# Moving the on-chip tiles of a two-layer encoder to multiples of 512 bytes, and attention's value tiles to 320 bytes apart

## The chip, the cores and the metric

The kernel runs on one core of a Trainium2 chip. The metric is the device time of one execution in microseconds (us); three runs of the kernel before gave 4280.89, 4287.06 and 4291.22 us, so the median is 4287.06 us. The core has TensorE (matrix products, "PE", its weight loads "PEld"), VectorE ("DVE"), ScalarE ("ACT"), GpSimd ("POOL") and SyncE ("SP", which here issues most transfers). All tiles spoken of lie in the core's on-chip memory, which has 128 partitions; a tile has the same byte address in each partition, and "address" below means that one.

## The reference

Two layers, each of this form, over 2048 tokens of width 1024, all in float32:

```
h    = rmsnorm(x, norm_w[l])
proj = h @ w_in[l]                                  # 1024 -> 3344 columns
y_dn = deltanet(qkv, z, b, a)                       # 5-tap convolution, 4 heads of 128, both directions
y_at = attention(q, k, v, z)                        # 8 query heads, 2 key/value heads of 64, rotary positions
x    = x + concat(y_dn, y_at) @ w_out[l]            # 1024 -> 1024
```

and a last rmsnorm. The attention has softmax over all 2048 keys.

## The kernel before, in words

The kernel holds activations transposed: features on the partitions, tokens along them. It has three kinds of stages with products 512 tokens wide, and they make most of its TensorE work. In all three a float32 operand is split into a rounded part ("hi", type fp32r) and the rest ("lo", fp32r too), and three products (hi·hi, hi·lo, lo·hi) are summed in a bank of the accumulator memory.

1. **Input projection** (`input_projection`, line L328 of the profile). 26 weight tiles of 1024 x 128 a layer. For each tile and each half of the tokens, 8 k-steps of three terms, each term two products of 128x128 weights (`w_hi` or `w_lo`, "stationary") with 128x512 of `h_hi` or `h_lo` ("moving"): 96 products a tile. Tile 0 is done at lines L304 and L311, together with 128x32 weights `ba_w` for the gates. Beside it VectorE does the convolution (L516, L518) and the rotary products (L553 to L570), ScalarE evacuates (L408), GpSimd squares (L381), and TensorE sums squares between its products (L339, 448 pairs of small products over both layers).
2. **DeltaNet** (`delta_net`, L1039, L1047, L1064, L1072, L1115). A chunked recurrence over 16 chunks of 128 tokens in both directions. Its products are plain float32, 128 columns wide, and depend on each other across engines.
3. **Attention** (`attention`). 32 blocks a layer, each of 512 queries of one head. A block has 8 pairs of key tiles; TensorE does, for a pair, 4 score products (L1655 with `k1`, L1656 with `k2` of 68 rows, moving `q1`, `q2`), 6 value products (L1673: stationary `v_hi` or `v_lo`, 128x65, moving `p_hi` or `p_lo`), and 2 products for the next block's row maximum (L1628: stationary `q1`, moving `k1`). One small transpose (L1644) is added: 96 wide products and 1 small one a block. VectorE reads the maxima (L1743), splits the probabilities (L1761), and once a block does L1749, L1755 and L1767. ScalarE takes the exponential (L1730) and rounds (L1734).
4. **Output projection** (`output_projection`, L1890 and L1904). Products with the same shapes and types as those of L328: 128x128 weights `w_hi`/`w_lo`, moving 128x512 of `y_hi`/`y_lo`, two in a row with the same weights.

The order of all work is written out by hand; engines meet by semaphores. A max unit (L1628) may start when VectorE has read the unit two before it, since there are two banks for them.

Where a tile lies is decided by the order in which the tiles are made: each is put behind the last, its size rounded up to 32 bytes. The persistent tiles (`c_ident` and so on, in `build`) come first, the tiles of a stage behind them, and when a stage ends its room is used again. Before the change every fp32r product has its moving tile at a multiple of 64 bytes.

Of the kernel before, what the change touches and what calls it, by code (L numbers as in the profile page):

```python
# [7 lines left out]
P = 128  # L8
F32 = mybir.dt.float32
F32R = mybir.dt.float32r  # L10
# [4 lines left out]
SEQ = 2048  # L15
D_MODEL = 1024
DEPTH = 2
KT = D_MODEL // P
NC = SEQ // P
# [4 lines left out]
PADW = SEQ + CONV_K - 1  # L24
EPS = 1e-6

DN_HEADS = 4
N_DIR = 2
# [117 lines left out]
def input_projection(nc, a, c, l):  # L146
# [6 lines left out]
    with ExitStack() as stack, semaphores(nc, names) as s:  # L153
        b = Buffers(nc, stack, "proj")
        h_hi = b.sbuf("h_hi", [P, KT, SEQ], F32R)
        h_lo = b.sbuf("h_lo", [P, KT, SEQ], F32R)
        pad = b.sbuf("pad", [P, 2, PADW])
        out = b.sbuf("out", [P, 2, SEQ])
        w_raw = b.sbuf("w_raw", [P, 2, WCOLS])
        w_hi = b.sbuf("w_hi", [P, 2, KT, P], F32R)  # L160
        w_lo = b.sbuf("w_lo", [P, 2, KT, P], F32R)
        nw = b.sbuf("nw", [P, KT])
        sq = b.sbuf("sq", [P, SEQ])
        taps = b.sbuf("taps", [P, 2, WCOLS - KT * P])
        ba_raw = b.sbuf("ba_raw", [P, KT, W_BA])
        ba_w = b.sbuf("ba_w", [P, KT, 2 * W_BA], F32R)
        qk_w = b.sbuf("qk_w", [P, 6])
# [629 lines left out]
class Lanes:  # L797
# [3 lines left out]
    def __init__(self, b):  # L801
        self.raws = b.sbuf("lane_raw", [P, 2, BLK, BLK])
        self.mats = b.sbuf("lane_mat", [P, 2, BLK, BLK])
        self.invs = b.sbuf("lane_inv", [P, 2, BLK, BLK])
        self.tmp = b.sbuf("lane_tmp", [P, BLK * BLK // 4])
        self.beta = b.sbuf("lane_beta", [P, len(GROUP_STEPS), BLK])

# [27 lines left out]
def delta_net(nc, a, c, l):  # L835
# [6 lines left out]
    with ExitStack() as stack, semaphores(nc, names) as s:  # L842
# [9 lines left out]
                  for n in range(2))  # L852
        state = pair("state")
        norm = b.sbuf("norm", [P, 1])
        mean = b.sbuf("mean", [P, N_DIR, DN_HEADS])
        inv_mean = b.sbuf("inv_mean", [P, N_DIR, DN_HEADS])
        room = b.sbuf("room", [P, 12, N_DIR, DN_HEADS, P])
        r, se, oa, sq, ot, z, o, first_o, btc, y, am, kk = (room[:, n] for n in range(12))
# [656 lines left out]
K_ROWS = DH + NQ  # L1515


FIRST_BANKS = 6


def attention(nc, a, c, l):
# [15 lines left out]
    with ExitStack() as stack, semaphores(nc, names) as s:  # L1537
# [3 lines left out]
        v = b.sbuf("v", [P, NC, KV_HEADS, DH])  # L1541
        v_hi = b.sbuf("v_hi", [P, KV_HEADS, NC, DH + 1], F32R)
        v_lo = b.sbuf("v_lo", [P, KV_HEADS, NC, DH + 1], F32R)
        quarter = b.sbuf("quarter", [NQ, NQ, P])
# [10 lines left out]
        with nc.Block() as block:  # L1555
# [64 lines left out]
            def _(pe):  # L1620
# [38 lines left out]
                def values(j, slot, pair, first=False):  # L1659
# [9 lines left out]
                    for m in range(2):  # L1669
                        tile = 2 * pair + m  # L1670
                        for part_v, part_p in ((v_hi, p_hi), (v_hi, p_lo), (v_lo, p_hi)):
                            opens = tile == 0 and part_v is v_hi and part_p is p_hi
                            mm = nc.tensor.matmul(ps[0:DH + 1, 6 + kv, :], part_v[:, kv, tile, :], part_p[:, at, m, :],  # L1673
                                                  start=opens, stop=(tile == NC - 1 and part_v is v_lo))
# [379 lines left out]


FIRST_DIMS = [*range(0, DH // 4), *range(DH // 2, 3 * DH // 4)]
SECOND_DIMS = [d + DH // 4 for d in FIRST_DIMS]

# [31 lines left out]
def build(nc, a):  # L2090
# [6 lines left out]
    with ExitStack() as stack:  # L2097
        sb = lambda n, shape: stack.enter_context(nc.sbuf_tensor(n, shape, F32))
        c.ident = sb("c_ident", [P, P])
        c.ones = sb("c_ones", [P, P])  # L2100
        c.eps = sb("c_eps", [P, 2])
        c.quarters = sb("c_quarters", [P, 4])
        c.sums = sb("c_sums", [P, 2 * DN_HEADS, NC])
        c.tok = sb("c_tok", [P, TABLES, NC, ITEMS])
        c.v_scale = sb("c_v_scale", [P, NC, DN_HEADS])
        c.q_eps = sb("c_q_eps", [P, DN_HEADS, NC])
        c.sq_acc = sb("c_sq_acc", [P, SEQ])
        with semaphores(nc, "loaded set_up") as s:
# [88 lines left out]
```

## Time and profile before

| | |
|---|---|
| runs, median (lowest, highest) | 4287.06 (4280.89, 4291.22) us |
| span of the profiled execution, first to last instruction | 4274.5 us |
| what lies around the span, against the median | 12.6 us |
| TensorE busy | 3902.5 us, 91% of the span |
| VectorE, ScalarE, GpSimd busy | 2705.1, 1858.6, 671.4 us |
| mean granted TensorE clock | 0.956 |

No time is listed for the profiled execution other than its span. The profile gives each instruction's start and duration. For products the duration is a pipeline's latency and successive ones overlap, so what counts is the distance from one start to the next. In a timeline the same instructions in a row are merged: the start is that of the first, "x4" says how many. From the start of one row to the start of the next, divided by the count, is the distance.

### The profile page before, as it was taken

To read this page: it belongs to the slowest core of one execution; us is meant where nothing else is said; L and a number is where in the kernel's file an instruction comes from. 1 tells how busy PE (TensorE), PEld (TensorE's weight loads), DVE (VectorE), ACT (ScalarE), POOL (GpSimd) and SP (SyncE) were. 2 spreads that over 40 slices of the span, in tenths; PEclk is the share of its full clock that TensorE was granted. 3 is DMA by queue.
4 is the path that set the end of the run, shared out by engine and by line. 5 is a ranking of instruction groups with operands and counts; after the bars stand their busy time and mean duration, and the time that the engine had idled before them with its cause. 6 is when DMAs were issued, how large, how long until landed. Compare 5 with 4: busy or idle time off the path is not lost. (4 is left out here: it accounts for less than half of the span.)

```text
span 4274.5 us, 57577 instructions
## 1 busy us (share of the span) xinstructions
PE 3902.5 (91%) x19722; PEld 3081.4 (72%) x19722; DVE 2705.1 (63%) x3343; ACT 1858.6 (43%) x2599; POOL 671.4 (16%) x760
## 2 busy tenths in 40 slices
PE   4999998769979999998989999966997999999996
PEld 3788886569956666666768888855997666666674
DVE  5553035557779999985255420726776999999743
ACT  3222111335547777772133211112553777777611
POOL 0011100387510000000000111015864000000000
PEclk9999999889989999999989999988998999999997
DMA  6112145645550000005232121745455200000245
GB/s 248 67 59 74 59 152 187 159 104 141 144 164 25 23 25 23 22 14 175 113 113 74 59 74 59 237 128 130 130 154 145 109 25 23 25 22 24 67 161 221
DMA packets 338168, 423.04 MB, mean 99 GB/s; under 512 B 106248, under 2 KB 255880, under 8 KB 315600
## 3 DMA queue, kind: packets, MB, share of 16 engines
q1 hardware_dynamic: 335120, 399.93, 30.0%
q10 hardware_dynamic: 2880, 20.97, 1.2%
q8 instruction: 94, 1.54, 0.2%
q14 instruction: 74, 0.61, 0.0%
HBM read 272.89 MB, written 147.91 MB: 98 GB/s over the span
## 5 line engine op out<-in xcount | busy, mean ns | idle before, releaser
L1743 DVE TENSOR_REDUCE att_sb_part<-att_banks 128x1 f32<-128x512 f32 x992 | 681.1, 687 | 108.9 <-PE att_banks L1628 101.4
L1730 ACT ACTIVATE att_sb_probs<-att_banks 128x1024 f32<-128x1024 f32 x512 | 525.0, 1025 | 320.6 <-PE att_banks L1656 320.4
L1761 DVE TENSOR_TENSOR att_sb_p_lo<-att_sb_probs,att_sb_p_hi 128x1024 fp32r<-128x1024 f32 x512 | 622.3, 1215 | 19.1 <-ACT att_sb_p_hi L1734 18.9
L1734 ACT ACTIVATE att_sb_p_hi<-att_sb_probs 128x1024 fp32r<-128x1024 f32 x512 | 543.6, 1062 | 16.2
L328 PE MATMUL proj_banks<-proj_sb_h_hi,proj_sb_w_hi 128*128 128x512 f32 x1600 | 519.9, 406 | 6.2 <-DVE proj_sb_w_lo L476 6.2
L328 PE MATMUL proj_banks<-proj_sb_h_lo,proj_sb_w_hi 128*128 128x512 f32 x1600 | 516.7, 404 | 0.0
L328 PE MATMUL proj_banks<-proj_sb_h_hi,proj_sb_w_lo 128*128 128x512 f32 x1600 | 516.6, 404 | 0.0
L1039 PE MATMUL dn_banks<-dn_sb_room 128*128 128x128 f32 x3072 | 378.3, 283 | 57.4 <-DMA dn_sb_room<-proj 24.9
L1039 PEld LDWEIGHTS dn_banks<-dn_sb_room 128*128 128x128 f32 x3072 | 366.4, 198 | 79.8 <-DMA dn_sb_room<-proj 34.9
L1656 PE MATMUL att_banks<-att_sb_q,att_sb_k 68*128 68x512 f32 x1024 | 409.4, 400 | 0.0
L1655 PE MATMUL att_banks<-att_sb_q,att_sb_k 128*128 128x512 f32 x1024 | 407.6, 398 | 1.9 <-DVE att_sb_q L1755 1.9
L1673 PE MATMUL att_banks<-att_sb_p_hi,att_sb_v_hi 128*65 128x512 f32 x1024 | 404.1, 395 | 1.4 <-DVE att_sb_p_lo L1761 1.4
L1673 PE MATMUL att_banks<-att_sb_p_hi,att_sb_v_lo 128*65 128x512 f32 x1024 | 403.4, 394 | 0.0
L1673 PE MATMUL att_banks<-att_sb_p_lo,att_sb_v_hi 128*65 128x512 f32 x1024 | 402.9, 393 | 0.0
L1628 PE MATMUL att_banks<-att_sb_k,att_sb_q 128*128 128x512 f32 x992 | 400.2, 405 | 1.4 <-DVE att_sb_part L1743 1.4
L381 POOL TENSOR_TENSOR proj_sb_sq<-proj_sb_out 128x2048 f32<-128x2048 f32 x28 | 100.8, 3600 | 1882.9 <-ACT proj_sb_out L424 1316.9
L328 PEld LDWEIGHTS proj_banks<-proj_sb_h_hi,proj_sb_w_hi 128*128 128x128 f32 x1600 | 290.6, 190 | 65.4 <-issue 7.1
L328 PEld LDWEIGHTS proj_banks<-proj_sb_h_lo,proj_sb_w_hi 128*128 128x128 f32 x1600 | 292.6, 190 | 61.3
L328 PEld LDWEIGHTS proj_banks<-proj_sb_h_hi,proj_sb_w_lo 128*128 128x128 f32 x1600 | 292.4, 190 | 61.2
L476 DVE TENSOR_TENSOR proj_sb_w_lo<-proj_sb_w_raw,proj_sb_w_hi 128x1024 fp32r<-128x1024 f32 x52 | 69.0, 1327 | 412.2 <-ACT proj_sb_w_hi L403 412.2
L408 ACT ACTIVATE proj_sb_out<-proj_banks 128x1024 f32<-128x1024 f32 x56 | 57.5, 1026 | 545.3 <-PE proj_banks L328 545.3
L1628 PEld LDWEIGHTS att_banks<-att_sb_k,att_sb_q 128*128 128x128 f32 x992 | 189.8, 191 | 78.3 <-DVE att_sb_part L1743 5.1
(236 smaller groups left out, 5645.3 us busy)
## 6 DMA issues: line engine op xcount, KB each, us to landing
proj<-proj_sb_out SPq DMA_DIRECT2D x40, 1024.0 KB, 4.6
dn_sb_kq<-proj SPq DMA_DIRECT2D x64, 512.0 KB, 5.3
proj_sb_w_raw<-in_w_in SPq DMA_DIRECT2D x52, 516.0 KB, 5.1
dn_sb_room<-proj SPq DMA_DIRECT2D x32, 768.0 KB, 5.3
att_sb_q<-att_q SPq DMA_DIRECT2D x64, 256.0 KB, 3.0
ahead_delta<-x_res SPq DMA_DIRECT2D x16, 1024.0 KB, 6.7
x_res<-ahead_delta SPq DMA_DIRECT2D x16, 1024.0 KB, 4.2
proj_sb_pad<-proj SPq DMA_DIRECT2D x24, 512.0 KB
```

What stands on the lines that cost most here:

```text
L328: mm = nc.tensor.matmul(ps[:, 2 * half + n, :], w[:, u, k, :], h[:, k, at:at + QB], start=(k == 0 and w is w_hi and h is h_hi), stop=(k == ...
L381: nc.gpsimd.tensor_tensor(sq[:], out[:, u, :], out[:, u, :], ALU.mult).then_inc(s["squared"], 1)
L476: nc.vector.tensor_tensor(w_lo[:, u].rearrange("p k m -> p (k m)"), w_raw[:, u, 0:KT * P], w_hi[:, u].rearrange("p k m -> p (k m)").bitcas ...
L1039: mm = nc.tensor.matmul(out[:, h, :], left[:, h, :], right[:, h, :], start=True, stop=True)
L1628: nc.tensor.matmul(ps[:, 4 + u % 2, :], q1[:, slot, tile * P:(tile + 1) * P], k1[:, slot % 2, keys * QB:(keys + 1) * QB], start=True, stop ...
L1655: nc.tensor.matmul(out, k1[:, slot % 2, keys], q1[:, slot, :], start=True, stop=False)
L1656: mm = nc.tensor.matmul(out, k2[:, slot % 2, keys], q2[:, slot, :], start=False, stop=True)
L1673: mm = nc.tensor.matmul(ps[0:DH + 1, 6 + kv, :], part_v[:, kv, tile, :], part_p[:, at, m, :], start=opens, stop=(tile == NC - 1 and part_v ...
L1730: nc.scalar.activation(probs[:, pair % 2], ps[:, 2 * (pair % 2):2 * (pair % 2) + 2, :], ACT.Exp, scale=SCALE).then_inc(s["exp_done"], 1)
L1734: nc.scalar.activation(p_hi[:, pair % SLOTS], probs[:, pair % 2], ACT.Copy).then_inc(s["hi_done"], 1)
L1743: nc.vector.tensor_reduce(part[:, w // NQ, w % NQ:w % NQ + 1], ps[:, 4 + w % 2, :], AX.X, ALU.max) \
L1761: nc.vector.tensor_tensor(p_lo[:, pair % SLOTS], probs[:, pair % 2], p_hi[:, pair % SLOTS].bitcast(F32), ALU.subtract).then_inc(s["lo_done ...
```

## The change

No instruction is added, taken away or put elsewhere: with line numbers left out, the lists of instructions of the two kernels, engine by engine, are the same, word for word. Only addresses change. The persistent tiles get two fillers, `c_front` and `c_back`, so that `c_ident` and each stage's first tile start at a multiple of 512; in the projection, DeltaNet and the persistent group, tiles with odd sizes go behind the large ones; and a value tile of 65 columns gets room for 80 (`V_ROOM`), of which 65 are used.

| tile (use) | address before | modulo 512, 64 | address after | modulo 512, 64 |
|---|---|---|---|---|
| `proj_sb_h_hi` (moving) | 29376 | 192, 0 | 30208 | 0, 0 |
| `proj_sb_h_lo` (moving) | 94912 | 192, 0 | 95744 | 0, 0 |
| `proj_sb_w_hi` (stationary) | 201504 | 288, 32 | 177664 | 0, 0 |
| `proj_sb_w_lo` (stationary) | 209696 | 288, 32 | 185856 | 0, 0 |
| `proj_sb_ba_w` (stationary) | 226688 | 384, 0 | 202240 | 0, 0 |
| `proj_sb_pad` (convolution) | 160448 | 192, 0 | 212032 | 64, 0 |
| `dn_sb_room` (both) | 177568 | 416, 32 | 177664 | 0, 0 |
| `dn_sb_kq`, `dn_sb_state` | 156992, 173376 | 320, 0 | 157184, 173568 | 0, 0 |
| `att_sb_k1`, `k2` (both; stationary) | 103104, 119488 | 192, 0 | 103936, 120320 | 0, 0 |
| `att_sb_q1`, `q2` (both; moving) | 162752, 170944 | 448, 0 | 167424, 175616 | 0, 0 |
| `att_sb_p_hi`, `p_lo` (moving) | 187328, 203712 | 448, 0 | 192000, 208384 | 0, 0 |
| `att_sb_v_hi`, tile t (stationary) | 144064 + 260 t | 64: 4 t | 144896 + 320 t | 64: 0 |
| `out_sb_y_hi`, `y_lo` (moving) | 103104, 168640 | 192, 0 | 103936, 169472 | 0, 0 |
| `out_sb_w_hi`, `w_lo` (stationary) | 201408, 209600 | 192, 0 | 202240, 210432 | 0, 0 |

The diff, cut:

```diff
@@ input_projection
         h_lo = b.sbuf("h_lo", [P, KT, SEQ], F32R)
-        pad = b.sbuf("pad", [P, 2, PADW])
         out = b.sbuf("out", [P, 2, SEQ])
-        w_raw = b.sbuf("w_raw", [P, 2, WCOLS])
         w_hi = b.sbuf("w_hi", [P, 2, KT, P], F32R)
         w_lo = b.sbuf("w_lo", [P, 2, KT, P], F32R)
+        sq = b.sbuf("sq", [P, SEQ])
+        ba_w = b.sbuf("ba_w", [P, KT, 2 * W_BA], F32R)
+        ba_raw = b.sbuf("ba_raw", [P, KT, W_BA])
+        w_raw = b.sbuf("w_raw", [P, 2, WCOLS])
+        pad = b.sbuf("pad", [P, 2, PADW])
         nw = b.sbuf("nw", [P, KT])
...
@@ Lanes, delta_net
-        self.beta = b.sbuf("lane_beta", [P, len(GROUP_STEPS), BLK])
+        self.beta = None
...
         state = pair("state")
+        room = b.sbuf("room", [P, 12, N_DIR, DN_HEADS, P])
+        lanes.beta = b.sbuf("lane_beta", [P, len(GROUP_STEPS), BLK])
         norm = b.sbuf("norm", [P, 1])
...
@@ attention
+V_ROOM = 80
...
-        v_hi = b.sbuf("v_hi", [P, KV_HEADS, NC, DH + 1], F32R)
-        v_lo = b.sbuf("v_lo", [P, KV_HEADS, NC, DH + 1], F32R)
+        v_hi = b.sbuf("v_hi", [P, KV_HEADS, NC, V_ROOM], F32R)
+        v_lo = b.sbuf("v_lo", [P, KV_HEADS, NC, V_ROOM], F32R)
...
-                            mm = nc.tensor.matmul(ps[0:DH + 1, 6 + kv, :], part_v[:, kv, tile, :], part_p[:, at, m, :],
+                            mm = nc.tensor.matmul(ps[0:DH + 1, 6 + kv, :], part_v[:, kv, tile, 0:DH + 1], part_p[:, at, m, :],
...
@@ build
+FRONT_WORDS, BACK_WORDS = 96, 112
...
+        sb("c_front", [P, FRONT_WORDS])
         c.ident = sb("c_ident", [P, P])
         c.ones = sb("c_ones", [P, P])
+        c.sq_acc = sb("c_sq_acc", [P, SEQ])
...
+        sb("c_back", [P, BACK_WORDS])
```

## Rows read from the trace of the kernel before

**Rows 1.** The page's first part: busy us, share of the span, instructions.

```profile
span 4274.5 us, 57577 instructions
PE 3902.5 (91%) x19722; PEld 3081.4 (72%) x19722; DVE 2705.1 (63%) x3343; ACT 1858.6 (43%) x2599; POOL 671.4 (16%) x760
```

**Rows 2.** Busy time by stretch: projection, DeltaNet, attention, output projection (layer 1).

```profile
core 0: us, PE busy (x) PEld busy (x) DVE busy (x) ACT busy (x) POOL busy (x), PEclk, DMA share, GB/s
114.00:732.00 618.00, 613.60 (x2850) 504.28 (x2850) 250.43 (x199) 115.59 (x102) 50.41 (x14) 0.99 0.29 100
762.00:1190.00 428.00, 362.84 (x2880) 339.59 (x2880) 276.88 (x490) 182.31 (x607) 280.59 (x360) 0.93 0.52 137
1190.00:1935.00 745.00, 727.89 (x3104) 503.78 (x3104) 668.29 (x865) 545.72 (x522) 4.55 (x4) 0.98 0.14 41
2028.00:2119.00 91.00, 91.00 (x403) 75.39 (x402) 24.73 (x17) 11.90 (x8) 0.00 (x0) 1.00 0.30 115
```

**Rows 3.** TensorE's waits: engine line <- what ended them, us, times, longest.

```profile
PE dn_banks L1039 <- DMA c_sq_acc<-d_blk: 36.3, 5, 16.7
PE dn_banks L1039 <- DMA dn_sb_room<-proj: 24.9, 13, 3.9
PE proj_banks L328 <- DVE proj_sb_w_lo L476: 6.2, 2, 3.1
PE dn_banks L1072 <- DMA dn_sb_kq<-proj: 5.0, 2, 3.2
PE att_banks L1628 <- DVE att_sb_part L1743: 1.4, 4, 0.4
```

**Rows 4.** Timeline of TensorE in the input projection: start us, us, what, count.

```profile
149.64 0.63 PE L328 MATMUL proj_banks<-proj_sb_h_hi,proj_sb_w_hi 128*128 128x512 f32 x2
...
155.73 0.63 PE L328 MATMUL proj_banks<-proj_sb_h_lo,proj_sb_w_hi 128*128 128x512 f32 x2
```

**Rows 5.** The same in the output projection.

```profile
2049.99 0.62 PE L1904 MATMUL out_banks<-out_sb_y_hi,out_sb_w_hi 128*128 128x512 f32 x2
...
2055.43 0.62 PE L1904 MATMUL out_banks<-out_sb_y_hi,out_sb_w_hi 128*128 128x512 f32 x2
```

**Rows 6.** How many L328 products there are: one of its three groups.

```profile
L328 PE MATMUL proj_banks<-proj_sb_h_hi,proj_sb_w_hi 128*128 128x512 f32 x1600 | 519.9, 406 | 6.2 <-DVE proj_sb_w_lo L476 6.2
```

**Rows 7.** Timeline of VectorE in attention, once a block, two blocks in a row.

```profile
1505.31 0.68 DVE L1755 TENSOR_TENSOR att_sb_q<-att_banks,att_sb_quarter 4x512 fp32r<-4x512 f32 x1
...
1527.75 0.68 DVE L1755 TENSOR_TENSOR att_sb_q<-att_banks,att_sb_quarter 4x512 fp32r<-4x512 f32 x1
```

**Rows 8.** Timeline of TensorE in attention around the block's small product.

```profile
1504.04 0.28 PE L1644 MATMUL att_banks<-c_ident,att_sb_top 128*4 128x128 f32 x1
1504.07 0.48 PE L1628 MATMUL att_banks<-att_sb_k,att_sb_q 128*128 128x512 f32 x1
1504.39 0.39 PE L1655 MATMUL att_banks<-att_sb_q,att_sb_k 128*128 128x512 f32 x1
```

**Rows 9.** Timeline of VectorE in attention, some of a block; idle time in brackets.

```profile
1501.78 0.69 DVE L1743 TENSOR_REDUCE att_sb_part<-att_banks 128x1 f32<-128x512 f32 x1
1502.50 0.17 DVE L1749 TENSOR_REDUCE att_sb_top<-att_sb_part 128x4 f32<-128x16 f32 x1
1502.85 0.69 DVE L1743 TENSOR_REDUCE att_sb_part<-att_banks 128x1 f32<-128x512 f32 x1 [0.18 <-PE att_banks L1628]
1503.46 1.22 DVE L1761 TENSOR_TENSOR att_sb_p_lo<-att_sb_probs,att_sb_p_hi 128x1024 fp32r<-128x1024 f32 x1
1504.59 0.69 DVE L1743 TENSOR_REDUCE att_sb_part<-att_banks 128x1 f32<-128x512 f32 x1
...
1516.46 0.68 DVE L1767 COPY att_sb_o<-att_banks 65x512 f32<-65x512 f32 x1
1517.06 0.68 DVE L1743 TENSOR_REDUCE att_sb_part<-att_banks 128x1 f32<-128x512 f32 x1
```

**Rows 10.** Timeline of TensorE in DeltaNet: products within `room`, then `kq` with `state`.

```profile
999.81 5.19 PE L1039 MATMUL dn_banks<-dn_sb_room 128*128 128x128 f32 x45
1004.84 3.40 PE L1039 MATMUL dn_banks<-dn_sb_state,dn_sb_kq 128*128 128x128 f32 x29
```

**Rows 11.** VectorE: durations of one operation by tile, min/median/max ns.

```profile
L518 DVE SCALAR_TENSOR_TENSOR proj_sb_out<-proj_sb_pad,proj_sb_taps,proj_sb_out x96: 2350/2352/2353, 116.6 to 2487.6; 128x2048 f32<-128x2048 f32 x96
...
L2035 DVE SCALAR_TENSOR_TENSOR fin_sb_x<-fin_sb_x,fin_sb_w,fin_sb_r x8: 2346/2347/2352, 4245.1 to 4261.0; 128x2048 f32<-128x2048 f32 x8
```

More of the change, by code:

```diff
@@ L156, in input_projection @@
         h_lo = b.sbuf("h_lo", [P, KT, SEQ], F32R)
-        pad = b.sbuf("pad", [P, 2, PADW])
         out = b.sbuf("out", [P, 2, SEQ])
-        w_raw = b.sbuf("w_raw", [P, 2, WCOLS])
         w_hi = b.sbuf("w_hi", [P, 2, KT, P], F32R)
         w_lo = b.sbuf("w_lo", [P, 2, KT, P], F32R)
+        sq = b.sbuf("sq", [P, SEQ])
[3 more added lines that the diff above has]
+        pad = b.sbuf("pad", [P, 2, PADW])
         nw = b.sbuf("nw", [P, KT])
-        sq = b.sbuf("sq", [P, SEQ])
         taps = b.sbuf("taps", [P, 2, WCOLS - KT * P])
-        ba_raw = b.sbuf("ba_raw", [P, KT, W_BA])
-        ba_w = b.sbuf("ba_w", [P, KT, 2 * W_BA], F32R)
         qk_w = b.sbuf("qk_w", [P, 6])
@@ L856, in delta_net @@
         inv_mean = b.sbuf("inv_mean", [P, N_DIR, DN_HEADS])
-        room = b.sbuf("room", [P, 12, N_DIR, DN_HEADS, P])
         r, se, oa, sq, ot, z, o, first_o, btc, y, am, kk = (room[:, n] for n in range(12))
@@ L2098, in build @@
         sb = lambda n, shape: stack.enter_context(nc.sbuf_tensor(n, shape, F32))
+        sb("c_front", [P, FRONT_WORDS])
         c.ident = sb("c_ident", [P, P])
         c.ones = sb("c_ones", [P, P])
+        c.sq_acc = sb("c_sq_acc", [P, SEQ])
+        c.tok = sb("c_tok", [P, TABLES, NC, ITEMS])
+        c.sums = sb("c_sums", [P, 2 * DN_HEADS, NC])
+        c.v_scale = sb("c_v_scale", [P, NC, DN_HEADS])
+        c.q_eps = sb("c_q_eps", [P, DN_HEADS, NC])
         c.eps = sb("c_eps", [P, 2])
         c.quarters = sb("c_quarters", [P, 4])
[L2103 to L2107, printed above, removed]
+        sb("c_back", [P, BACK_WORDS])
         with semaphores(nc, "loaded set_up") as s:
```

## The prediction

> **What bounds the kernel now.** I read the page's busy shares first, then the stretches, then the waits of TensorE, and last the timelines for the distance between products. TensorE is busy for 91% of the span [rows 1]. By stretch the reader sees that it is all but full in the projection (613.6 of 618 us), the attention (727.9 of 745) and the output projection (91 of 91), and has holes only in DeltaNet (362.8 of 428) [rows 2]. Its waits inside the projection and the attention are small: 6.2 us for L328 and 1.4 us for L1628 over both layers [rows 3]. So in these stages the time is the number of products times their distance, and a change that alters no instruction can act there only by altering the distance.
>
> **The distance in the two projections.** From 149.64 to 155.73 us the input projection starts 26 products (13 rows of two): 6.09 / 26 = 234.2 ns each [rows 4]. From 2049.99 to 2055.43 us the output projection starts 24: 5.44 / 24 = 226.7 ns [rows 5]. The granted clock is full in both (0.99 and 1.00, which is the level of 2.4 GHz), shapes and types are equal, both alternate between two banks with the same weights twice. What differs is where things lie: the moving tiles are at 192 modulo 512 in both, the weights at 192 in the output projection, at 288 in the input projection, which is no multiple of 64. This comparison is what the forecast rests on: 7.5 ns a product are there to be had, and the change puts the weights of L328 in the same relation to the moving tile that L1904 has today.
>
> **The sum, part by part.**
>
> *Input projection.* L328 has three groups of 1600 products, 4800 in all [rows 6]. 4800 x 7.5 ns = 36.0 us. Some of the distances hold a small product L339 between them and may save less; I take 35 us. Bounds: at no gain 0; if the new place were worse by as much as it could be better, +36; below, the moving tiles at 0 modulo 512 might also help, which no row shows, since every fp32r moving tile lies at 192 or 448 now. 512 columns at one a cycle of 2.4 GHz are 213.3 ns, so the lowest end is 4800 x 20.9 = 100 us. I take the value of the nearest row, L1904. The cover of the other engines holds: VectorE is busy 250 and ScalarE 116 of the 618 us [rows 2], and TensorE hardly waits for either.
>
> *Attention.* A block takes 1527.75 - 1505.31 = 22.44 us [rows 7]. It has 96 wide products and one small one; the small one and the wide one behind it take 4.39 - 4.04 = 0.35 us together [rows 8], so the small one adds about 0.12 us and the distance of the others is (22.44 - 0.12) / 96 = 232.5 ns. That lies above 226.7 too. Here the tiles differ in two ways: the value tiles start at 4 t modulo 64, so nearly all of them at no multiple of 64, and `k1` and `q1` are 256 bytes apart modulo 512. After the change all starts are multiples of 64. At 226.7 ns a block would take 96 x 0.2267 + 0.12 = 21.88 us, 0.56 us less; over 64 blocks 35.8 us. What is late next is VectorE. Back to back it needs for a pair 0.61 (maximum to split) + 1.13 (split to maximum) + 0.72 us [rows 9], for eight pairs 19.7 us, and once a block 0.17 (L1749), 0.68 (L1755) and 0.60 us (L1767) [rows 7, 9], 21.1 us in all. So it stays below 21.88, but where L1749 and L1755 come in neighbouring pairs it works without a pause, and TensorE running ahead can meet it there. I take off 4 us for that and count 32 us. Bounds: 0, if 65-column and 68-row weights are what costs the time and not their address; VectorE's 21.1 us a block caps the gain at 1.3 x 64 = 84 us; and above, +37 by the third rival.
>
> *Output projection.* Weights and moving tiles move together from 192 to 0 modulo 512. Nothing in their relation or in the multiple of 64 changes: 0. Bounds by the same two ends as above, for 1152 products of L1904: -15 us (13.4 ns each) to +9 (7.5 ns each).
>
> *DeltaNet.* Its products are plain float32. Within `room` (32 modulo 64) 45 of them take 1004.84 - 999.81 = 5.03 us, 111.8 ns each, and those of `kq` with `state` (multiples of 64) take 3.40 us for 29, the last one's length included, so no more than that [rows 10]. The address makes no difference there today, so I count 0.
>
> *Transfers.* The waits in which a transfer is named last are 36.3, 24.9 and 5.0 us, all in DeltaNet [rows 3]. Their tiles now start at multiples of 512. No row shows a transfer to such a place, so the bounds are a quarter of these waits either way, 17 us; most of the wait is for issue and landing and not for the moving itself, and I count 0. The Trainium skill (DMA: Bandwidth & Descriptors, How a descriptor splits into AXI transactions) says that a descriptor which does not start at a multiple of 256 bytes fetches from the boundary below and pays for the unused bytes; for a 512-byte piece at 320 it would give 18 beats in place of 16, a small gain, and no row here tells it apart from none.
>
> *VectorE, ScalarE.* The convolution L518 reads `pad` at all five shifts of 4 bytes and takes 2350 to 2353 ns; an operation of the same kind and size on an aligned tile, L2035, takes 2347 [rows 11]. So 5 ns at most hang on the address, off the path: 0.
>
> Sum: 35 + 32 = 67 us. The profiled execution's span of 4274.5 us becomes about 4208; with the 12.6 us that lie between span and median, 4287 - 67 = 4220 us.
>
> **The rivals.**
>
> *A: only the input projection gains.* Attention's products differ from L1904's in shape: 65 columns, 68 rows, other weights each time, several into one bank in a row. If that makes the 5.8 ns, the address does not help. For it: the score products too, whose weights are at multiples of 64 today, are part of a block at 232.5 ns. Against: they stand between value products whose weights are not. 4287 - 35 = 4252 us.
>
> *B: only whole small lines count, so the projection gains nothing.* If a start at any multiple of 16 bytes is as good as another, 288 is no worse than 192, and only the value tiles at 4 t gain: 4287 - 32 = 4255 us. The difference between 234.2 and 226.7 ns would then need another cause. The Trainium skill (Advanced Engine Details and Errata, Memory Cachelines) has such a rule: lines of 16 bytes, at least two hits on each. By it the weights at 288 are fine, and rows 4 and 5 speak against it as the whole story.
>
> *C: slower.* All streams that TensorE reads, and those of the other engines, now start in step modulo 512. If two streams in step collide, the products of both stages get slower; the mechanism would show as a distance of L328 above 234.2 ns, and from there on it decides. Price, if it adds what the change was to save: +36 us in the projection, +37 in attention, 4360 us; half of it 4323. Against: the output projection has its weights and its moving tiles in step today and is the fastest.
>
> *D: no change.* The distances keep their values, since something other than the address makes them (banks, order of issue): within 8 us of 4287.
>
> *E: larger.* Moving tiles at a multiple of 512 stream faster than any does today. Half way to 213.3 ns: projection 4800 x 14.2 = 68, output 1152 x 6.7 = 8, attention 6144 x 12.5 = 77 us, which VectorE's cap of 84 just allows: 4134 us.
>
> **Chances.** Forecast, both stages: 0.45. A: 0.20. B: 0.03. C: 0.12. D: 0.12. E: 0.08. The forecast is 4220 us. The range is 4175 to 4284 us: it takes in A, B and the better half of D, and leaves out C, most of E and the rest of D, together about 0.2. The likeliest case's own range is 4205 to 4240. What can be told from no change is about 0.2% of 4287, 8.6 us. Faster: 0.45 + 0.20 + 0.03 + 0.08 = 0.76. Same: 0.12. Slower: 0.12.
>
> **What would show it.** Right: in the timeline of the changed kernel two rows of L328 products 26 products apart are 5.89 us apart and not 6.09; L1755 comes every 21.9 to 22.0 us; L1904 stays at 226.7 ns; DeltaNet's stretch keeps its 428 us; and VectorE's idle time before L1743 falls. A shows as L1755 still every 22.4 us; C as L328 above 234.2 ns; E as L1904 below 226.7. The forecast is wrong if L328 stays at 234 ns: then the address of the weights was not what sets the two projections apart.

## The result, and the profile after

The changed kernel took 4243.31 us (median of 4 runs, 4241.96 to 4246.30), the kernel before 4286.06 us (4 runs, 4280.89 to 4291.22). The ratio is 0.9913, 95% interval [0.9897, 0.9930], so it is faster by 43 us. The forecast was 67 us less, 4220 us; the range of 4175 to 4284 us holds the time. One term of the sum came as worked out, the other did not.

Between the two profiled executions the spans differ by only 32 us (4274.5 and 4242.5). Part of the gap to 43 us lies in the choice of the execution before. Wherever both numbers of an execution are on record, its time is 1.7 to 3.8 us above its span (4244.30 and 4242.5 us for the profiled one after). So the profiled execution of before took an estimated 4277 us, some 9 us less than the median of 4286. The 12.6 us that the prediction puts between span and median are mostly this, and not time around the span. The kernel before ran again beside the experiments and had medians of 4277.5 to 4281.5 us there.

The first view is the busy time by stretch, each cut from its first to its last TensorE product, layer 1: after (projection, DeltaNet, attention, output projection), then before for two of them. The columns are those of [rows 2].

```profile
48.00:711.80 663.80, 650.18 (x3050) 537.32 (x3050) 291.24 (x226) 139.85 (x120) 50.42 (x14) 0.99 0.30 107
751.50:1170.80 419.30, 363.34 (x2880) 340.63 (x2880) 275.18 (x489) 181.25 (x606) 276.41 (x357) 0.93 0.49 136
1183.30:1914.70 731.40, 723.78 (x3104) 504.31 (x3104) 663.92 (x864) 546.09 (x522) 4.72 (x2) 0.98 0.13 40
1922.20:2111.10 188.90, 180.93 (x768) 147.20 (x768) 81.71 (x49) 34.56 (x23) 0.00 (x0) 0.97 0.45 151
```

```profile
48.00:728.10 680.10, 666.62 (x3050) 539.55 (x3050) 291.44 (x226) 139.72 (x120) 50.41 (x14) 0.99 0.30 104
...
1197.10:1932.60 735.50, 727.89 (x3104) 503.77 (x3104) 664.13 (x864) 545.72 (x522) 4.34 (x2) 0.98 0.13 40
```

The counts and the granted clock are the same; TensorE's busy time fell, by 16.4 us in the projection and by 4.1 in the attention. Both layers, in us (the layer-2 values are cut in the same way):

| stretch | before, layers 1 and 2 | after, layers 1 and 2 | difference |
|---|---|---|---|
| input projection | 680.1, 679.5 | 663.7, 663.8 | -32.1 |
| DeltaNet | 416.3, 419.7 | 419.3, 416.7 | 0.0 |
| attention | 735.4, 734.2 | 731.3, 731.1 | -7.2 |
| output projection | 187.5, 187.0 | 188.9, 194.3 | +8.7 |

These and the short stretches between them make the 32 us of the spans. The +8.7 us are no distance between products: TensorE's waits, before and then after, show that the wait of the output projection for `ahead_gates` was longer (columns as in [rows 3]).

```profile
PE out_banks L1890 <- DVE ahead_gates L1943: 12.0, 6, 2.9
```

```profile
PE out_banks L1893 <- DVE ahead_gates L1946: 17.2, 6, 4.6
```

That accounts for 5.2 of the 8.7 us. In the experiments below the output projection's stretch is anywhere from 187.0 to 194.6 us, in kernels laid out as before and as after. So I take it as variation. Projection and attention together give 39.3 us, between the 32 of the spans and the 43 of the medians.

The timeline of TensorE in the input projection, which answers to [rows 4], and in the output projection, which answers to [rows 5]:

```profile
148.97 0.61 PE L328 MATMUL proj_banks<-proj_sb_h_hi,proj_sb_w_hi 128*128 128x512 f32 x2
...
154.86 0.62 PE L328 MATMUL proj_banks<-proj_sb_h_lo,proj_sb_w_hi 128*128 128x512 f32 x2
...
2041.53 0.62 PE L1907 MATMUL out_banks<-out_sb_y_hi,out_sb_w_hi 128*128 128x512 f32 x2
...
2046.97 0.62 PE L1907 MATMUL out_banks<-out_sb_y_hi,out_sb_w_hi 128*128 128x512 f32 x2
```

26 products of L328 take 5.89 us (226.5 ns each; 6.09 and 234.2 before), 24 of the output projection 5.44 us, as before. In the attention the same operation of VectorE as in [rows 7], two blocks in a row:

```profile
1512.36 0.68 DVE L1758 TENSOR_TENSOR att_sb_q<-att_banks,att_sb_quarter 4x512 fp32r<-4x512 f32 x1
...
1534.65 0.68 DVE L1758 TENSOR_TENSOR att_sb_q<-att_banks,att_sb_quarter 4x512 fp32r<-4x512 f32 x1
```

A block takes 22.29 us. That is 0.15 less than the 22.44 before, where about 0.5 was forecast. The timeline of TensorE within one pair shows where it stays slow:

```profile
1514.20 0.39 PE L1658 MATMUL att_banks<-att_sb_q,att_sb_k 128*128 128x512 f32 x1
1514.43 0.39 PE L1659 MATMUL att_banks<-att_sb_q,att_sb_k 68*128 68x512 f32 x1
1514.66 0.40 PE L1658 MATMUL att_banks<-att_sb_q,att_sb_k 128*128 128x512 f32 x1
1514.89 0.40 PE L1659 MATMUL att_banks<-att_sb_q,att_sb_k 68*128 68x512 f32 x1
1515.13 0.40 PE L1631 MATMUL att_banks<-att_sb_k,att_sb_q 128*128 128x512 f32 x1
```

From the first of these to the fifth it is 0.93 us, 232.5 ns each, though all tiles start at multiples of 512. In these four the weights have 128 and 68 rows in turn. Averaged over the whole execution the score products come at 233.1 ns (233.9 before) and the value products at 228.7 to 230.1 (231.1 to 231.7 before). Means of this kind, here and below, are over distances between 200 and 260 ns of one kind of product.

### The profile page after: what moved, and what is told of

Read it like the earlier page. It is cut to its first block and busy times, and to the rows that moved or that the text cites. A ratio compares the mean times of both kernels' runs of the same rounds, so it can differ in the third digit from the quotient of the medians.

```text
span 4242.5 us, 57577 instructions
## 1 busy us (share of the span) xinstructions
PE 3863.7 (91%) x19722; PEld 3079.8 (73%) x19722; DVE 2702.6 (64%) x3343; ACT 1859.4 (44%) x2599; POOL 671.6 (16%) x760
## 5 line engine op out<-in xcount | busy, mean ns | idle before, releaser
L1746 DVE TENSOR_REDUCE att_sb_part<-att_banks 128x1 f32<-128x512 f32 x992 | 680.7, 687 | 101.2 <-PE att_banks L1631 87.3
L328 PE MATMUL proj_banks<-proj_sb_h_hi,proj_sb_w_hi 128*128 128x512 f32 x1600 | 510.9, 401 | 6.3 <-DVE proj_sb_w_lo L476 6.3
L328 PE MATMUL proj_banks<-proj_sb_h_lo,proj_sb_w_hi 128*128 128x512 f32 x1600 | 507.4, 398 | 0.0
L328 PE MATMUL proj_banks<-proj_sb_h_hi,proj_sb_w_lo 128*128 128x512 f32 x1600 | 507.2, 398 | 0.0
L328 PEld LDWEIGHTS proj_banks<-proj_sb_h_hi,proj_sb_w_hi 128*128 128x128 f32 x1600 | 289.7, 190 | 57.1 <-issue 7.1
L328 PEld LDWEIGHTS proj_banks<-proj_sb_h_lo,proj_sb_w_hi 128*128 128x128 f32 x1600 | 291.6, 189 | 52.5
L328 PEld LDWEIGHTS proj_banks<-proj_sb_h_hi,proj_sb_w_lo 128*128 128x128 f32 x1600 | 291.6, 189 | 52.3
```

Of the source, the lines that this page charges most:

```text
L328: mm = nc.tensor.matmul(ps[:, 2 * half + n, :], w[:, u, k, :], h[:, k, at:at + QB], start=(k == 0 and w is w_hi and h is h_hi), stop=(k == ...
L1746: nc.vector.tensor_reduce(part[:, w // NQ, w % NQ:w % NQ + 1], ps[:, 4 + w % 2, :], AX.X, ALU.max) \
```

## The experiments

Theory 1 ("address"): the start of a tile decides, so all wide products should come to 226.7 ns. Theory 2 ("relation and shape"): weights and moving tile must start at the same place modulo some size ("in step"), and the shape must not change from product to product. The rival for the attention is that only the shape matters there. Each ratio below is to runs of the kernel before that were taken beside the experiment.

**m1_table: 24 series of 60 products, nothing beside them.**

```diff
+for n, (ws, ms, rows, cols, same_bank) in SECTIONS.items():
+    for i in range(COUNT):
+        r, c = rows[i % len(rows)], cols[i % len(cols)]
...
+        mm = nc.tensor.matmul(ps[0:c, bank, :], w[n][0:r, at:at + c], m[n][0:r, mo:mo + QB], start=True, stop=True)
```

> A table of distances and not the encoder: 24 series of 60 products, 128x512 moving, fp32r, with chosen starts of the weights (w) and the moving tile (m) in bytes modulo 512, and chosen rows and columns; the input is copied to the output, and nothing else of the reference is computed. Theory 'multiple of 64': 226.7 ns wherever the weights start at 0, 64, 192 or 256, whatever the moving tile's start (also w0_m32, w192_m448), and about 234 for weights at 32 (w32_m0, w32_m32, w288_m192) and at 4, 8, 16, 48. Rival 'in step modulo 512': 226.7 only for w0_m0, w32_m32 and w192_m192, and 231 to 238 for all others. Rival 'lines of 16 bytes': 226.7 for w16, w32, w48, and more only for w4 and w8. For attention: theory 'rows': rows68 or rows128_68 above 230 and cols65, cols128_65, same_bank at 226.7; rival 'columns': the reverse; rival 'same bank': same_bank above 230.

Single series cut out of TensorE's timeline (the line is the same for all of them): weights at 64 and then at 256 modulo 512 with the moving tile at 0; both at 32; weights at 288 with the moving tile at 192, which are the places of L328 before; and both at 192.

```profile
145.63 14.16 PE L2161 MATMUL banks<-m_w_m,w_w_m 128*128 128x512 f32 x60
...
159.63 13.77 PE L2161 MATMUL banks<-m_w_m,w_w_m 128*128 128x512 f32 x60
...
200.99 13.78 PE L2161 MATMUL banks<-m_w_m,w_w_m 128*128 128x512 f32 x60
...
214.60 14.21 PE L2161 MATMUL banks<-m_w_m,w_w_m 128*128 128x512 f32 x60
...
228.65 13.80 PE L2161 MATMUL banks<-m_w_m,w_w_m 128*128 128x512 f32 x60
```

With about 0.4 us for the last product's length, 13.77 us are 59 distances of 226.6 ns, and 14.16 us of 233.2. Weights at 64 are slow, weights at 256 are not; both at 32 are fast. So "a multiple of 64" is not the rule. Mean of the last 40 distances of each series, in ns:

| weights, moving (bytes modulo 512) | ns |
|---|---|
| 0, 0; 256, 0; 32, 32; 192, 192; 192, 448 | 226.7 |
| 4, 0 / 8, 0 / 16, 0 | 232.4 / 230.7 / 233.3 |
| 32, 0; 48, 0; 64, 0; 0, 32 | 233.3 |
| 0, 64 | 228.9 |
| 288, 192 | 234.3 |

And the shapes, everything at 0: three series of the timeline, with 68 rows always, then 128 and 68 rows in turn, then 128 rows by 65 columns.

```profile
255.88 13.77 PE L2161 MATMUL banks<-m_rows,w_rows 68*128 68x512 f32 x60
...
269.49 14.17 PE L2161 MATMUL banks<-m_rows,w_rows 128*128 128x512 f32 x60
...
323.11 14.31 PE L2161 MATMUL banks<-m_cols,w_cols 128*65 128x512 f32 x60
```

68 rows all the time run at 226.7 ns, 128 and 68 in turn at 233.3, 65 columns at 235.0 where the weights are 512 bytes apart, at 233.0 where they are 260 apart and at 233.2 for 320. 128 and 96 rows in turn come at 233.3 as well, 128 and 65 columns in turn at 233.5. Theory 2 holds for the table. All of these series go to two banks in turn; one that goes to a single bank comes at 226.7 ns, so the bank is not the cause (it does not sum products there, as the attention does).

**e1_rows128: the changed kernel with `k2` and `q2` filled up to 128 rows.**

```diff
+FULL_ROWS = P
...
-k2 = b.sbuf("k2", [K_ROWS, KV_HEADS, SEQ], F32R)
+k2 = b.sbuf("k2", [FULL_ROWS, KV_HEADS, SEQ], F32R)
...
-q2 = b.sbuf("q2", [K_ROWS, SLOTS, QB], F32R)
+q2 = b.sbuf("q2", [FULL_ROWS, SLOTS, QB], F32R)
...
-nc.vector.memset(k2[DH:K_ROWS, :, :].bitcast(F32), 1.0).then_inc(s["k2_ones"], 1)
+nc.vector.memset(k2[DH:FULL_ROWS, :, :].bitcast(F32), 1.0).then_inc(s["k2_ones"], 1)
+nc.vector.memset(q2[DH:FULL_ROWS, :, :].bitcast(F32), 0.0).then_inc(s["k2_ones"], 1)
...
```

> The changed kernel, but the second score product of attention has 128 rows, not 68: the 60 new rows hold ones in k2 and zeros in q2. Theory 'the 68-row products knock TensorE out of its even distance': all 96 wide products of a block come at 226.7 ns, the block takes 21.9 us, not 22.29, and the time falls by 64 x 0.4 = 25 us against the changed kernel, to about 4218 us. Rival '65 columns or neighbours of other shape do it': the block stays at 22.2 to 22.3 us and the time at 4243.

4215.78 us (4 runs), ratio to the kernel before 0.9865 [0.9838, 0.9891]. The timeline, from the end of one block's value products over four score products to the next value products:

```profile
1511.63 0.39 PE L1677 MATMUL att_banks<-att_sb_p_hi,att_sb_v_lo 128*65 128x512 f32 x1
...
1512.53 0.39 PE L1632 MATMUL att_banks<-att_sb_k,att_sb_q 128*128 128x512 f32 x1
1512.76 0.39 PE L1659 MATMUL att_banks<-att_sb_q,att_sb_k 128*128 128x512 f32 x1
...
1513.44 0.39 PE L1660 MATMUL att_banks<-att_sb_q,att_sb_k 128*128 128x512 f32 x1
...
1513.90 0.40 PE L1677 MATMUL att_banks<-att_sb_p_hi,att_sb_v_hi 128*65 128x512 f32 x1
...
1514.84 0.39 PE L1677 MATMUL att_banks<-att_sb_p_lo,att_sb_v_hi 128*65 128x512 f32 x1
```

From 1512.53 to 1513.44 it is 0.91 us for four. The score products are at 227.3 ns on average, and a block takes 22.05 us, not the 21.9 that I expected. TensorE multiplies zeros and is faster for it. A large part of what the attention did not gain by the change was the alternation of rows.

The value products show something that Theory 2 does not allow. They are 65 columns wide throughout, and their tiles, 320 bytes apart, start at 0, 64, 128 and 192 modulo 256 in turn, while the moving tile starts at 0. The four from 1511.63 (the end of tile 14 and tile 15, at 128 and 192) take 0.90 us, about 226 ns each; the four from 1513.90 (tiles 0 and 1, at 0 and 64) take 0.94 us, 235 ns each. Over the whole execution the means are, by start:

| value tile starts at, modulo 256 | 0 | 64 | 128 | 192 |
|---|---|---|---|---|
| e1, ns | 234.3 | 230.1 | 227.1 | 226.8 |
| changed kernel, ns | 231.7 | 230.8 | 228.2 | 227.5 |

So for 65 columns the same place as the moving tile is the slow one, which agrees with the 235.0 ns of the table, and 128 or 192 bytes past it they are as fast as the products in step. The table's series with tiles 320 apart (0, 64 and 128) is slower, 233.2 ns, than the mean of these three, so neighbours seem to count too. What the kernel shows is that 65 columns cost nothing by themselves, and that what a place costs differs between 65 and 128 columns.

**e2_before_w64: the kernel before, its projection's weights moved by 32 bytes.**

```diff
+b.sbuf("fill", [P, 8])
 w_raw = b.sbuf("w_raw", [P, 2, WCOLS])
```

> The kernel before with one tile of 32 bytes put ahead of the projection's weights, so that w_hi and w_lo start at 320 modulo 512 (a multiple of 64, 128 past the moving tile's 192) and not at 288. Theory 'multiple of 64': L328 comes at 226.7 ns, each projection is 16 us shorter, the time about 4286 - 33 = 4253 us. Rival 'in step modulo 512': L328 stays at 231 to 234 ns and the time within 10 us of 4286.

4270.27 us (10 runs), ratio 0.9988 [0.9975, 1.0002]. The weights now start at 320, a multiple of 64, against the moving tile's 192:

```profile
149.66 0.64 PE L329 MATMUL proj_banks<-proj_sb_h_hi,proj_sb_w_hi 128*128 128x512 f32 x2
...
155.70 0.63 PE L329 MATMUL proj_banks<-proj_sb_h_lo,proj_sb_w_hi 128*128 128x512 f32 x2
```

6.04 us for 26, 232.3 ns: a start at a multiple of 64 gives a quarter of what was to be had, and the reason that my prediction named is wrong. The time's interval reaches 1, so the distance decides here and not the time.

**e3_v260: the changed kernel, its value tiles 260 bytes apart again, in the same room.**

```diff
-v_hi = b.sbuf("v_hi", [P, KV_HEADS, NC, V_ROOM], F32R)
-v_lo = b.sbuf("v_lo", [P, KV_HEADS, NC, V_ROOM], F32R)
+v_room = [b.sbuf(n, [P, KV_HEADS * NC * V_ROOM], F32R) for n in ("v_hi", "v_lo")]
+v_hi, v_lo = (r[:, 0:KV_HEADS * NC * (DH + 1)].rearrange("p (k c d) -> p k c d", k=KV_HEADS, d=DH + 1)
+              for r in v_room)
```

> The changed kernel with the value tiles 260 bytes apart again, in the same room. If the spacing is what moved attention's block from 22.44 to 22.29 us: 22.44 here and the span 4242.5 + 64 x 0.15 = 4252 us. If it was k1 and q1 coming into step: 22.29 us and the span unchanged.

4248.41 us in one run, which settles nothing by its time. The blocks alternate between 22.35 and 22.44 us with the two key/value heads, whose value tiles start 64 bytes apart modulo 256:

```profile
1486.11 0.68 DVE L1759 TENSOR_TENSOR att_sb_q<-att_banks,att_sb_quarter 4x512 fp32r<-4x512 f32 x1
...
1508.46 0.68 DVE L1759 TENSOR_TENSOR att_sb_q<-att_banks,att_sb_quarter 4x512 fp32r<-4x512 f32 x1
...
1530.89 0.68 DVE L1759 TENSOR_TENSOR att_sb_q<-att_banks,att_sb_quarter 4x512 fp32r<-4x512 f32 x1
```

Neither of the two values that I expected came: one head's blocks lost all of the 0.15 us, the other's about 0.07. On average the spacing of the value tiles is worth 0.11 us a block, most of the small gain. This is not quite the kernel before in its value tiles: there `v_lo` starts 128 bytes from `v_hi` modulo 256, here at the same place.

**m2_table: a second table.** The kernel is that of m1_table with other series.

> A second table of distances and not the encoder, of the same form as the first. The first gave 226.7 ns where weights and moving tile start at the same place modulo 256 (w0_m0, w256_m0, w32_m32, w192_m192, w192_m448), and 229 to 234 elsewhere. Theory 'in step modulo 256': w0_m256, w4_m4 and w128_m128 at 226.7; w96, w128, w192, w224, w240 with m0, w320_m192 and w0_m128 above 228. Rival 'modulo 128': w128_m0, w0_m128 and w320_m192 at 226.7 too. Shapes: theory 'any weights of fewer than 128 columns fall out of step': cols127, cols96, cols64 and cols32 above 230; rival 'only a count that is no multiple of 32': cols96, cols64 and cols32 at 226.7. Theory 'a change of the row count costs, a constant one doesn't': rows64 and rows32 at 226.7 (as rows68 was), rows128_127 at 233 (as 128/68 and 128/96 were); rows128_64 again at 429 and rows128_32 near it, if what costs there is the change to a quarter or half of the array. 'again' at 226.7 shows that the clock held.

```profile
89.14 13.90 PE L2161 MATMUL banks<-m_w_m,w_w_m 128*128 128x512 f32 x60
...
102.88 14.16 PE L2161 MATMUL banks<-m_w_m,w_w_m 128*128 128x512 f32 x60
...
116.88 13.76 PE L2161 MATMUL banks<-m_w_m,w_w_m 128*128 128x512 f32 x60
...
171.96 14.17 PE L2161 MATMUL banks<-m_w_m,w_w_m 128*128 128x512 f32 x60
```

These are weights at 192, 224 and 240 with the moving tile at 0, and both at 4.

| series (weights, moving, or shape with both at 0) | ns |
|---|---|
| 128, 128; 0, 256; 240, 0 | 226.7 |
| 96, 0 / 128, 0 / 192, 0 / 224, 0 | 234.3 / 232.4 / 228.9 / 233.4 |
| 0, 128; 320, 192 | 232.2; 232.6 |
| 4, 4 | 233.3 |
| 127, 96, 64, 32 columns | 233.4, 230.0, 230.2, 231.7 |
| 64 rows throughout | 226.7 |
| 128 and 127 rows in turn; 128 and 65; 128, 128, 68, 68; 128, 128, 128, 68 | 233.3 each |

128 bytes between the two is not enough (232.4), 256 is: the size is 256. Two series don't fit "the same place modulo 256": both at 4, which is slow, and weights 16 below the moving tile (240 against 0), which is fast. All distances in this table were taken at a granted clock of 1.00. The series with 32 rows, and those with 128 and 64 or 32 rows in turn, ran wholly or mostly with the clock at its lower level, so that what I expected of 32 rows throughout stays open; the last section tells of them. In both tables only the distance between the two starts, modulo 256, decides the value for 128x128 weights, to within 0.4 ns and with the one exception of both at 4: 288 against 192 gives what 96 against 0 gives, and 0 against 64 what 192 against 0 gives.

**e4_all128: e1, and value tiles of 128 columns, 512 bytes apart.**

```diff
-V_ROOM = 80
+V_ROOM = P
...
-mm = nc.tensor.matmul(ps[0:DH + 1, 6 + kv, :], part_v[:, kv, tile, 0:DH + 1], part_p[:, at, m, :],
+mm = nc.tensor.matmul(ps[:, 6 + kv, :], part_v[:, kv, tile, :], part_p[:, at, m, :],
```

(cut: the columns above 65 are zero; `v` shares room with `ahead_w`, `o` and `quarter` with `c_sq_acc`)

> e1_rows128 with value tiles of 128 columns too, 512 bytes apart (columns 65 to 127 hold zeros; v, o and quarter share room with tiles that are idle in attention). Every wide product of attention is then 128x128 by 128x512, in step. Theory 'rows and columns both knock it out of step': all 96 at 226.7 ns, block 21.9 us against e1's 22.05, time 64 x 0.17 = 11 us below e1_rows128, about 4205 us. Rival 'what is left in e1 comes from something else (VectorE, semaphores)': block 22.05 us and the time that of e1.

4218.16 us (4 runs), ratio 0.9852 [0.9831, 0.9873]. Two blocks of the timeline of VectorE, then one of them by busy time (TensorE, its weight loads, VectorE, ScalarE, GpSimd):

```profile
1486.03 0.68 DVE L1760 TENSOR_TENSOR att_sb_q<-att_banks,c_sq_acc 4x512 fp32r<-4x512 f32 x1
1507.94 0.68 DVE L1760 TENSOR_TENSOR att_sb_q<-att_banks,c_sq_acc 4x512 fp32r<-4x512 f32 x1
1529.85 0.68 DVE L1760 TENSOR_TENSOR att_sb_q<-att_banks,c_sq_acc 4x512 fp32r<-4x512 f32 x1
```

```profile
1486.03:1507.94 21.91, 21.91 (x99) 18.02 (x98) 20.74 (x27) 16.73 (x16) 0.00 (x0) 1.00 0.08 24
```

A block takes 21.91 us, and all wide products are at 226.9 to 227.5 ns. This is the block that I forecast for the change alone (21.88). VectorE is busy 20.74 of it and does not stop TensorE. The 0.14 us against e1 lie in the value tiles that started at 0 and 64 there (24 products a block, 232.2 ns on average in e1 and 226.7 here). e4 changes their columns and their places in one, so it does not tell whether another place alone would have done; that was not tried. The attention's stretches are 722.3 and 718.0 us, 29 us less than before. Against e1 the time of the whole is the same within the intervals, where I had expected 11 us less, 4205 us; in e4's profiled execution 5 us went to the output projection's stretch of layer 1 (194.4 us against 189.1 in e1). The attention takes 7.6 us less than in e1.

**e5_w96: the changed kernel, 96 bytes put ahead of the projection's weights.**

```diff
+b.sbuf("fill", [P, 24])
 w_hi = b.sbuf("w_hi", [P, 2, KT, P], F32R)
```

> The changed kernel with 96 bytes of room ahead of the projection's weights: w_hi and w_lo start 96 past the moving tile modulo 256, as in the kernel before, all else as changed. Theory 'the relation of weights and moving tile makes the projection's gain': L328 at 234.3 ns again, each projection 16 us longer, the time 32 us above the changed kernel, about 4275. Rival 'something else in the new order of tiles made it': the time stays near 4243.

4271.66 us (10 runs), ratio 0.9985 [0.9972, 0.9998]. 26 products take 6.10 us again, and the projection's stretches are 680.3 and 680.5 us, those of the kernel before, while a block of attention stays at 22.29:

```profile
149.43 0.64 PE L329 MATMUL proj_banks<-proj_sb_h_lo,proj_sb_w_hi 128*128 128x512 f32 x2
...
155.53 0.63 PE L329 MATMUL proj_banks<-proj_sb_h_hi,proj_sb_w_lo 128*128 128x512 f32 x2
```

One filler takes back the projection's whole gain. It also moves the tiles behind the weights; e8 below moves them too and keeps the gain. So the gain is the relation between weights and moving tile and nothing else of the change.

**e6_all32: the changed kernel, each stage's tiles at 32 modulo 512.**

```diff
-FRONT_WORDS, BACK_WORDS = 96, 112
+FRONT_WORDS, BACK_WORDS = 96, 120
```

> The changed kernel with 32 bytes more in c_back: every stage's tiles start 32 bytes past a multiple of 512, still in step with each other, none at a multiple of 64. Theory 'only the relation counts': L328 at 226.7 ns, block 22.29 us, time 4243 within 0.2%. Rival 'multiples of 64 (or 512) count': L328 at 230 or more and the time 15 to 35 us longer.

4245.44 us (4 runs), ratio 0.9923 [0.9906, 0.9940]; 26 products in 5.90 us:

```profile
149.56 0.62 PE L328 MATMUL proj_banks<-proj_sb_h_hi,proj_sb_w_hi 128*128 128x512 f32 x2
...
155.46 0.61 PE L328 MATMUL proj_banks<-proj_sb_h_lo,proj_sb_w_hi 128*128 128x512 f32 x2
```

The multiple of 512 itself brings nothing. It makes sure that the projection's tiles stand in step.

**e7_before_rows128: the kernel before, with the 128 rows of e1 alone.**

```diff
-k2 = b.sbuf("k2", [K_ROWS, KV_HEADS, SEQ], F32R)
+k2 = b.sbuf("k2", [P, KV_HEADS, SEQ], F32R)
-q2 = b.sbuf("q2", [K_ROWS, SLOTS, QB], F32R)
+q2 = b.sbuf("q2", [P, SLOTS, QB], F32R)
...
```

(cut: the new rows are filled as in e1)

> The kernel before, with its own places, and only k2 and q2 filled up to 128 rows (ones against zeros, so the sums stay). In it the score products' weights and moving tiles already start at the same place modulo 256 (256 apart modulo 512); the value products' do not, and stay 65 columns wide. Theory (both conditions must hold: same place modulo 256, and no change of shape between products): the score products come to about 227 ns, the value products stay at 231 to 232, L328 stays at 234. A block then falls from 22.44 by about 64 x 6 ns = 0.38 us less what the value products and VectorE take back, so to 22.1 to 22.2; two layers 16 to 22 us, the ratio 0.995 to 0.996. Rival (rows matter only once the tiles stand at multiples of 512, or the gain of the padded rows in the changed kernel was of another kind): the block stays within 0.05 us of 22.44 and the ratio is 1.000 +- 0.002.

4265.19 us (5 runs), ratio 0.9963 [0.9949, 0.9976]. A block takes 22.20 us:

```profile
1501.67 0.68 DVE L1755 TENSOR_TENSOR att_sb_q<-att_banks,att_sb_quarter 4x512 fp32r<-4x512 f32 x1
1523.87 0.68 DVE L1755 TENSOR_TENSOR att_sb_q<-att_banks,att_sb_quarter 4x512 fp32r<-4x512 f32 x1
```

The score products come at 229.6 ns, so the 227 that I expected was too low; the value products are at 230.5 to 231.2. The same products are at 227.3 in e1, where only the places differ, so a product's distance seems to hang on its neighbours too; that was not tried. The rival, that the rows count only at the new places, falls. The two effects add up, as the blocks' medians show (us):

| | 68 rows, 65 columns | 128 rows, 65 columns | 128 rows, 128 columns |
|---|---|---|---|
| places before | 22.44 | 22.20 | not tried |
| places after | 22.29 | 22.05 | 21.91 |

**e8_w240: the changed kernel, 240 bytes ahead of the projection's weights.**

```diff
+b.sbuf("fill", [P, 60])
 w_hi = b.sbuf("w_hi", [P, 2, KT, P], F32R)
```

> The changed kernel with 240 bytes ahead of the projection's w_hi, so its weights start at 240 modulo 256 and the moving tiles at 0; nothing else of the computation changes. In the table of products alone, weights at 240 against a moving tile at 0 came at 226.7 ns, while 224 came at 233.4 and 192 at 228.9. If the table carries over to the kernel, L328 stays at 227 to 228 ns and the time is that of the changed kernel, 4243 us (ratio 0.992). If only the very same place modulo 256 will do, L328 comes at about 234 ns, as with 96 bytes, and the time is about 4270 us (ratio 0.9985).

4237.34 us (4 runs), ratio 0.9897 [0.9881, 0.9912], which overlaps the changed kernel's own. 26 products take 5.89 us:

```profile
149.14 0.61 PE L329 MATMUL proj_banks<-proj_sb_h_lo,proj_sb_w_hi 128*128 128x512 f32 x2
...
155.03 0.62 PE L329 MATMUL proj_banks<-proj_sb_h_hi,proj_sb_w_lo 128*128 128x512 f32 x2
```

The table carries over to the kernel. For 128x128 weights "the same place modulo 256" is therefore sufficient in all that I tried but the pair at 4, but not necessary: weights 16 bytes below are as good. For weights of 65 columns it is not sufficient (e1). Why is open.

## Why the prediction was right in one term and wrong in the other

*What bounds the kernel.* Right: no instruction moved, the clock stayed, and the gain is in the distance between TensorE's products, 39.3 us over the two stages. In this pair of profiles the output projection's longer waits took some of it back.

*Input projection, 35 us.* Right in size: 32.1 us in the profiles, 226.5 ns in place of 234.2, and L1904 was the right row to take the price from. Averaged over the kernel the distance fell from 233.9 to 227.3 ns, by 6.6 and not by 7.5, which is the missing 3 us. The reason given beside it had two parts. "No multiple of 64" is wrong (e2: 320 is one and gives 232.3 ns; both at 32 in e6 give 226.9). "The same relation as L1904 has" is right (e5 takes the gain back, e6 keeps it). That the forecast came out in spite of the wrong half is partly luck: the change put the weights at a multiple of 64 and in step at once. With a multiple of 64 alone, as in e2, the projection's stretches are 675.9 and 676.2 us, 7.5 us less than before and not 32.

*Attention, 32 us.* Right in sign, wrong in size: 7 us by the stretches, or 0.15 us x 64 = 10 us by the typical block. The step that failed is "at 226.7 ns a block would take 21.88 us", which gave all of the 5.8 ns to the address. The term was 32 us, and 7 to 10 were measured. Of the 0.53 us that a block can lose, the change's places give 0.15 and constant rows (in place of 128 and 68 in turn) 0.24, by the table of blocks above. The last 0.14 came with value tiles of 128 columns at multiples of 512; they hang on the 65 columns and the place together. "After the change all starts are multiples of 64" was true and not the point: at 320 bytes apart half of the value tiles start at 0 or 64 modulo 256, the slow places for 65 columns (e1). The prediction had this as its lower bound ("65-column and 68-row weights are what costs the time") and as rival A with a chance of 0.20, and named the evidence for it: the score products had their weights at multiples of 64 and were slow all the same. The value of a mixed group had been taken from one mean (232.5 ns) over three shapes. That row could not tell them apart, and the weight should have gone more to A. With A's 4252 us and the forecast of 4220, the measured 4243 lies nearer to A. The range of 4175 to 4284 us holds it because it was drawn wide enough for A and B, not because the attention was understood. Of what A names, constant rows and full columns matter. Other weights each time and several products into one bank do not: in e4 both are as before, and all wide products are at 226.9 to 227.5 ns.

*VectorE as the next limit, 4 us off.* The change did not make blocks short enough to test it, and where e4 does, it is wrong. There TensorE's waits for the maxima (L1633 for L1748) are 5.3 us in all, against 1.4 before, which looks like the 4 us. But all six lie in the first 26 us of an attention stage, its opening; in the blocks of 21.91 us TensorE is busy throughout and waits for nothing. The likeness of the numbers is chance. The rows of the waits after the change, and then in e4:

```profile
PE att_banks L1631 <- DVE att_sb_part L1746: 1.6, 5, 0.4
```

```profile
PE att_banks L1633 <- DVE att_sb_part L1748: 5.3, 6, 1.7
```

*VectorE's idle time before L1743* fell from 108.9 to 101.2 us, the way that was named.

*Output projection, DeltaNet, transfers, 0 each.* Right within the spread: the output projection's products stayed at 226.7 ns; DeltaNet's stretches changed by +3.0 and -3.0 us. The waits in which a transfer is named last are 68.6 us in all, 66.2 before, too little a difference to tell from none.

*Rivals B, C, D, E.* B fell with the projection, and in the table weights at 16, 32 or 48 against 0 cost 233.3 ns. C (streams in step collide) fell for 128x128 weights, where in step is the fast case; the 65-column value tiles in step are the slow ones, 234.3 ns in e1. E fell: moving tiles at a multiple of 512 give 226.7 ns, no less, and so do both tiles at 32 or at 192 in the first table. D fell with the result.

The best kernel among those run is e1 (4215.78 us), level with e4 (4218.16): the placement, and score products of 128 rows throughout. Against the kernel before that is 1.3 to 1.5%.

## What to carry to other kernels

Where a profile shows equal products at two distances, first compare weights' and moving tile's starts with each other, not with a round number, and then look whether the shape changes from one product to the next. For weights narrower than 128 columns split the products by where their tile starts: the good place is not the same as for full ones. A mean over a mixed group is no price for any of its members: split it by shape and by place before an effect is given to one cause. Rows of zeros that keep the shape constant cost TensorE nothing here and gained more (0.24 us a block) than the placement (0.15).

## What the runs showed of the hardware that was not expected

- Alternating 128 and 64 rows took 429 ns a product at a granted clock of 1.00, almost twice the 233.3 ns of 128 with 68 or 96 rows, and of 128 with 127 rows in the second table. The row of the timeline for the 60 products:

```profile
297.50 25.68 PE L2161 MATMUL banks<-m_rows,w_rows 128*128 128x512 f32 x60
```

- In the second table the granted clock fell to its lower level during the series with 32 rows and stayed there through the next (0.50 from 294 to 336 us); 128 and 64 rows in turn then took 723 ns. The 32-row products had come at 226 to 236 ns until the clock fell, and at 426 to 427 after. 128 and 65 rows in turn, the next series, started at this level and came at 426 to 427 ns as well, and at 233.3 once the clock was back at 1.00. So the 6.6 ns that a change of the row count costs at full clock do not show at the lower one. 723 ns is 1.7 times the plain distance there, where at full clock 429 is 1.9 times.
- The slow distance is a pattern that repeats: in L328 before it was 232, 237, 238, 231, 234, 235, 233 ns, over and over, and the series of the second table with 96 bytes between weights and moving tile has the same values within 1 ns. What in the chip makes it was not tried.
